# A decoder block on one core: 32 tokens by gathered expert rows in place of 16, and another order of searches, masks and dots

## The reference

```python
scores = jnp.einsum('thpk,hpnk->thpn', q, sub_keys)
v1, i1 = lax.top_k(scores[:, :, 0], PEER_TOPK)
v2, i2 = lax.top_k(scores[:, :, 1], PEER_TOPK)
best, pos = lax.top_k(cand, PEER_TOPK)            # of the sums v1 + v2
experts = (e1 * N_KEYS + e2)
gates = jax.nn.softmax(best, axis=-1)
...
u = expert_u[ic]
a = jax.nn.gelu(jnp.einsum('cd,ced->ce', xc, u), approximate=False) * gc
v = expert_v[ic]
return jnp.einsum('ce,ced->cd', a, v)
```

## Time and profile before

| | us |
|---|---|
| median of 3 runs (1616.78 to 1618.3) | 1616.78 |
| span of the profiled execution | 1615.6 |
| PE busy in it | 1607.3 |
| DVE busy | 1283.2 |
| ACT busy | 690.3 |
| V stage, first to last product | 521.6 |

### The profile page before, as it was taken

How to read it: one execution, slowest core, us unless ns; L and a number is a source line. 1 busy time by engine, 2 the same in 40 slices (tenths; PEclk the granted TensorE clock), 3 DMA queues, 4 the chain that set the end, 5 groups by cost and what they waited for, 6 DMA issues and landing times.

```text
span 1615.6 us, 25174 instructions
## 1 busy us (share of the span) xinstructions
PE 1607.3 (99%) x8581; PEld 1422.2 (88%) x8581; DVE 1283.2 (79%) x2311; ACT 690.3 (43%) x921; POOL 373.4 (23%) x286
## 2 busy tenths in 40 slices
PE   9999999999999999999999999999999999999998
PEld 7888888888888999999999999998888888888887
DVE  6855733335557999998999998778998999999997
ACT  5323433333325433334666766433334333333333
POOL 0000000000000100003322223443453555454551
PEclk9999999999999999999999999999999999999999
DMA  4332332323321656659999999998999999999994
GB/s 176 125 103 92 117 104 91 104 91 104 105 90 54 231 180 201 208 192 337 319 365 366 377 354 377 414 360 322 391 413 363 407 414 398 412 409 403 411 362 163
DMA packets 126919, 424.34 MB, mean 263 GB/s; under 512 B 16384, under 2 KB 19472, under 8 KB 125200
## 3 DMA queue, kind: packets, MB, share of 16 engines
q1 hardware_dynamic: 75168, 232.85, 39.4%
q0 software_dynamic: 39264, 142.64, 22.9%
q10 hardware_dynamic: 12432, 48.26, 7.6%
HBM read 375.18 MB, written 48.51 MB: 262 GB/s over the span
## 4 chain that ended last, share of the span: by engine, by line
PE 99%; DMA 1%; ACT 0%; DVE 0%; SPq 0%; issue 0%; ACTq 0%
PE bank L920 21%; PE bank L922 20%; PE bank L921 20%; PE bank L1102 11%; PE bank L1104 11%; PE bank L1103 11%; PE bank L1080 3%; PE bank L986 1%; DMA h_t<-x_t 1%; PE bank L967 0%; PE bank L965 0%; PE bank L966 0%; PE bank L1116 0%; PE bank L1037 0%; PE bank L938 0%; PE bank L931 0%
## 5 line engine op out<-in xcount | busy, mean ns | idle before, releaser
L1155 DVE TENSOR_TENSOR w_lo<-w_raw,w_hi 128x1024 fp32r<-128x1024 f32 x347 | 424.2, 1222 | 156.6 <-ACT w_hi L589 151.5
L589 ACT ACTIVATE w_hi<-w_raw 128x1024 fp32r<-128x1024 f32 x347 | 366.7, 1058 | 395.7 <-PE bank L1104 259.5
L920 PE MATMUL bank<-xn_hi,w_hi 128*128 128x368 f32 (+1 forms) x1472 | 516.7, 351 | 0.1
L921 PE MATMUL bank<-xn_lo,w_hi 128*128 128x368 f32 (+1 forms) x1472 | 510.9, 347 | 0.0
L922 PE MATMUL bank<-xn_hi,w_lo 128*128 128x368 f32 (+1 forms) x1472 | 510.9, 347 | 0.0
L538 POOL DMA_INDIRECT rows<-u_rows,expert x128 | 160.8, 1256 | 953.2 <-DVE expert L1555 543.2
L1102 PE MATMUL bank<-w_hi,a_hi 128*128 128x512 f32 x768 | 298.9, 389 | 0.0
L1104 PE MATMUL bank<-w_hi,a_lo 128*128 128x512 f32 x768 | 298.8, 389 | 0.0
L1103 PE MATMUL bank<-w_lo,a_hi 128*128 128x512 f32 x768 | 298.8, 389 | 0.0
L920 PEld LDWEIGHTS bank<-xn_hi,w_hi 128*128 128x128 f32 x1472 | 276.2, 188 | 17.6 <-issue 0.6
L921 PEld LDWEIGHTS bank<-xn_lo,w_hi 128*128 128x128 f32 x1472 | 276.4, 188 | 17.4 <-issue 0.2
(11 more groups left out here) (224 smaller groups left out, 1381.7 us busy)
## 6 DMA issues: line engine op xcount, KB each, us to landing
w_raw<-u SPq DMA_DIRECT2D x128, 512.0 KB
w_raw<-v SPq DMA_DIRECT2D x128, 512.0 KB
g_dram<-g_sb ACTq DMA_DIRECT2D x12, 2048.0 KB, 11.0
g_in<-g_dram SPq DMA_DIRECT2D x84, 256.0 KB
act_dram<-act_out ACTq DMA_DIRECT2D x54, 384.0 KB
act_in<-act_dram SPq DMA_DIRECT2D x54, 384.0 KB
w_raw<-gate SPq DMA_DIRECT2D x32, 512.0 KB
w_raw<-w_in SPq DMA_DIRECT2D x31, 512.0 KB
```

Source lines behind the costliest of these rows:

```text
L589: act.activation(w_hi[:, slot, :], w_raw[:, slot, :], ACT.Copy).then_inc(hi_done, 1)
L920: pe.matmul(out, hi, x_hi, start=k == 0, stop=False)
L921: pe.matmul(out, hi, x_lo, start=False, stop=False)
L1155: dve.tensor_tensor(w_lo[:, slot, :], w_raw[:, slot, :], w_hi[:, slot, :].bitcast(F32), ALU.subtract).then_inc(lo_done, 1)
```

## The change

**More gathered tokens.** EXTRA becomes 32, so the product with u has 352 columns (DU, DENSE). xn_hi and xn_lo are written for these columns alone, and act_dram holds only them. There are 32 extra gathers in place of 16. x of the extra tokens is no longer laid out by ACT: PE transposes the last 128 tokens once (8 transposes after U0), ACT copies two halves to x_last, Pool writes them to HBM 16 times over (2.1 MB) and loads them in four groups of 512 KB, two at the start and two later.

**Searches.** The order of searches follows that of the scores: one more search and one more decode stand before the U stage (10 searches in it in place of 11), and the number of w_lo at each place comes from a table, SEARCHES, through a running count (`split_tiles`). The exponentials stand after 52 gelus in place of 50.

**Masks.** e2 is cut into 8 high and 16 low values; for 32 tokens at a time (BATCH) the one-hots of both are made (512 and 256 elements), the high one is multiplied with the gates, and the columns of a mask are the product of the two over 8 x 16 = 128 keys. The first equality of 2048 elements of each mask is gone. The last two masks have three parts.

**Dots.** 2 + 14 before the rounds in place of 5 + 13, ten a round in place of nine, 28 in the plain steps as before; 56 are left for the V stage in place of 44. The extra rows are rows 10 to 41 in place of 18 to 33, and their index is read back two rows after it was stored.

```diff
-EXTRA = 16
+EXTRA = 32
...
+BATCH = 2 * MASKED
+HIGH, LOW = 8, 16
...
-DOTS_BEFORE = (1, 1, 1, 1, 1, 1, 1, 2, 1, 1, 1, 1)
-DOTS_ROUND = (1, 1, 1, 1, 1, 1, 1, 2)
...
+SEARCHES = (((4, 1, 1, 0), 0, 0), ((1, 1, 1, 0), 2, 1), ((2, 1, 1, 0), 0, 0), ((1, 1, 1, 0), 3, 0),
...
+BEFORE_FIRST = EXP_AT
+DOTS_BEFORE = (1, 2, 2, 2, 2, 3, 2)
+DOTS_ROUND = (1, 1, 1, 2, 1, 1, 1, 2)
...
-EXTRA_FIRST = DOTS_TOPK * (TOPK_STEPS // 2 - 1) + sum(DOTS_BEFORE)
+EXTRA_FIRST = DOTS_TOPK + ROW_SLOTS + 4
...
+            pool.wait_ge(x_last_ready, 2)
+            pool.dma_start(x_rows_dram, x_last[P - EXTRA:, :].unsqueeze(1).broadcast_to([EXTRA, SPREAD, D])
+                           ).then_inc(x_rows_stored, 16)
+            pool.wait_ge(x_rows_stored, 16)
+            pool.wait_ge(job_done, AT_QUERY + HALVES)
+            for g in range(X_BUFFERS):
+                load_extra(g)
             pool.wait_ge(experts_ready, 1)
...
-                if q == EXTRA_SHOWN + ROW_SLOTS:
+                if q == EXTRA_SHOWN + 2:
                     pool.wait_ge(index_stored, 16)
...
-            for b in range(SLOTS // 2):
-                gelu_tile(TOPK_STEPS, b)
+            for m in range(EXP_AT // SLOTS * SLOTS, EXP_AT):
+                gelu_tile(m // SLOTS, m % SLOTS)
             act.wait_ge(shifted, 1)
...
+            u_tile(0, 0, xn_l)
+            pe.wait_ge(scores_ready, HALVES)
+            for k in range(2):
+                for j in range(SLOTS * k, SLOTS * (k + 1)):
+                    last = pe.transpose(bank[6 + k][:, (j - SLOTS * k) * P:(j - SLOTS * k + 1) * P],
+                                        xn_full[:, j, T - P:], ident[:])
+                last.then_inc(last_turned, 1)
...
             dve.wait_ge(scores_ready, SLOTS)
-            search(0, 0, (0, 0), of(q_split, 1))
+            search(0, 0, (0, 0), turns(1, 0, 1, 0))
+            search(1, 0, (1, 0), turns(0, 1, 0, 1))
             dve.wait_ge(scores_ready, 2 * SLOTS)
-            search(0, 1, (0, 1), of(q_split, 2))
-            decode(0, 0, 0, none)
-            search(1, 0, (1, 0), [none] * SLOTS)
+            search(0, 1, (0, 1), turns(1, 0, 1, 0))
+            decode(0, 0, 0, lambda: split_tiles(1))
+            search(1, 1, (1, 1), turns(0, 0, 1, 0))
...
+            def hot_parts(batch, gates, high, gated, low, parts):
+
+
+                tokens = slice(BATCH * batch, BATCH * (batch + 1))
+                highs, lows = [P, MASKED, HIGH, 2], [P, MASKED, LOW, 2]
+                chain.did(dve.tensor_tensor(low, iota_key[:, 0:LOW, :].unsqueeze(1).broadcast_to(lows),
+                                            lanes(e2_low[:, tokens], lows), ALU.is_equal))
...
+            def mask_columns(n, held, gated, low, parts):
+
+                half = slice(n % 2 * MASKED // 2, (n % 2 + 1) * MASKED // 2)
+                shape = [P, MASKED // 2, HIGH, LOW, 2]
+                chain.wait()
                 for k in range(parts):
...
+                    last = dve.tensor_tensor(
+                        held[:, 1 + k].rearrange("p s (a b) x -> p s a b x", b=LOW),
+                        gated[:, k, half].unsqueeze(3).broadcast_to(shape),
+                        low[:, half].unsqueeze(2).broadcast_to(shape), ALU.mult)
```

More of the change, by code:

```diff
@@ L276, in build @@
         rest = MemoryMap(nc, peer.at)
+        rest_at = rest.at
         act_out = rest("act_out", [P, SLOTS, DT])
@@ L1606, in mask_gates, with lanes @@
-            def mask_gates(n, gates, held, parts):
-                shape = [P, MASKED // 2, KEYS, 2]
-                dve.wait_ge(keys_masked, n + 1)
+            def lanes(tensor, shape):
+                return tensor.rearrange("p (s x) -> p s x", x=2).unsqueeze(2).broadcast_to(shape)
+            def hot_parts(batch, gates, high, gated, low, parts):
[3 more added lines that the diff above has]
+                                            lanes(e2_low[:, tokens], lows), ALU.is_equal))
+                chain.did(dve.tensor_tensor(high, iota_key[:, 0:HIGH, :].unsqueeze(1).broadcast_to(highs),
+                                            lanes(e2_high[:, tokens], highs), ALU.is_equal))
+                chain.wait()
+                for k in range(parts):
+                    chain.did(dve.tensor_tensor(gated[:, k], high, lanes(gates[:, k], highs), ALU.mult))
@@ L1629, in extra_gates, with masks_of, mask_half @@
                 chain.wait()
+            def masks_of(n):
+                if n < MASKS - MASKS_X:
+                    return masks[n % 2], gated_hot, low_hot[:], high_hot[:], GATE_PARTS
+                return masks_x[n % 2], gated_hot_x, low_hot_x, high_hot_x, EXTRA_PARTS
+            def mask_half(n, second):
+                held, gated, low, high, parts = masks_of(n)
+                if second:
+                    mask_columns(n, held, gated, low, parts)
+                    return
+                if n >= 2:
+                    dve.wait_ge(onehots_used, SLOTS * n)
+                mask_rows(slice(MASKED * n, MASKED * (n + 1)), held)
+                if n % 2 == 0:
+                    if n > 0:
+                        dve.wait_ge(masks_ready, n)
+                    if n < MASKS - MASKS_X:
+                        gates = gate_b[:, :, BATCH * (n // 2):BATCH * (n // 2 + 1)]
+                    else:
+                        gates = gate_x[:, :, MASKED * n - DU:MASKED * n - DU + BATCH]
+                    hot_parts(n // 2, gates, high, gated, low, parts)
             def dve_round(s):
@@ L1662, in _ @@
+            chain.did(dve.tensor_copy(e2_high[:], e2_shifted[:]))
+            chain.wait()
+            chain.did(dve.tensor_copy(e2_low[:], e2_int))
+            chain.wait()
+            mask_half(0, False)
+            split_tiles(1)
+            mask_half(0, True)
+            split_tiles(1)
+            u_dots(rows_done + sum(DOTS_BEFORE[:-1]), DOTS_BEFORE[-1])
             rows_done += sum(DOTS_BEFORE)
```

272 lines of the change are left out of this document (134 added, 138 removed).

## The result

The changed kernel takes **1627.26 us** (median of 4 runs, 1625.45 to 1628.14), the kernel before 1616.93 beside it: a ratio of 1.0061, 95% interval 1.0049 to 1.0073. It is 0.6% slower, and 20 us above the forecast of 1607.

The account below looks back on a forecast made before the run. TensorE (PE), busy 1607.3 of 1615.6 us, was taken to bound the kernel. From 1615.6, -20.5 - 0.9 + 0.9 + 8.8 + 2 gave 1605.9; with the median 1.2 above the span, 1607 us, range 1597 to 1615.

Parts of the forecast that it names:

- U tile 3.84 us, -20.5: U stage: 16 dense columns less make a PE tile 3.84 us in place of 4.0, -20.5 us over 128 tiles.
- transposes -0.9: PE: 16 transposes of the extra tokens become 8, at 0.8/7 us each, -0.9 us.
- third gate part +0.9: PE: a third gate part for 16 more tokens takes 16 products more, +0.9 us.
- Searches, cost 0: One search and decode move into the query stage's DVE idle time; w_lo of U8 stays about 1 us ahead.
- The first mask, 8.8 us (4 to 13): After tile U60 PE waits for mask 0: DVE needs 39.5 us plus 5 for late rows, against 35.5.
- clock +2 (0 to 4): Behind the wait at the first mask, PE's clock falls to half for a few us: +2 us.
- D: Rounds: one-hot product at half rate, 2.2 us in place of 1.14, makes the kernel slower, 1637 us; chance 0.07.
- Rounds covered: One-hot rounds: DVE's 36.5 us a round fit within PE's 38.4, so they cost nothing.
- Plain steps, cost 0: 28 dots in 16 tiles: DVE loses some 5 of its 9 us lead; cost 0, 3 if the DMA gives less.
- The rest is hidden: Copying x of the last tokens, stores of 352 columns and ACT's fewer layouts and copies add no time.
- V stage, cost 0: DVE busy 317 of 320 us, DMA at 418 GB/s: at their edge, 9.6 us of lead covering any loss.
- rival C: V stage or plain steps fall behind too, or U8 is late: 3 to 11 us more, 1610 to 1618; chance 0.22.

Follow-up runs that it names:

- the fifth slot: Changed kernel with one more slot for the rows of v, in scratch: 1624.7 us alone, 1613.0 us with 13 rows not gathered as well.

## Why the prediction was wrong, point by point

- **U tile 3.84 us, -20.5; transposes -0.9; third gate part +0.9:** right. U60 starts 11.0 us earlier, 9.6 + 0.9 by these terms and 0.4 for what PE had lost before; from U98 to V0 it is 3.9, as the terms have it.
- **Searches, cost 0:** right. w_lo of U8 is 2.0 us ahead (I had 1), and PE has no wait up to the mask.
- **The first mask, 8.8 us (4 to 13), clock +2 (0 to 4):** right in mechanism and size, 10.6 and 1.8. Counted from the end of U51 (720.4): the split 3.7 where I had 4.0, the subtraction 4.8 (5.2), w_hi 8.9 (9.3), the product of the softmax 16.3 (16.7), the dots 31.6 without waits for rows (31.5), the mask 7.7 (8.0). The waits for rows were 6.8, not 5. (39.5 and 5 are 44.5, not the 44.3 of the text; and with waits of 8.7 to 11.7 us from trace to trace, part of the match is luck.)
- **The product of one-hots at 1.14 (D, if half rate):** 1.22 us busy. D is out. **Rounds covered:** right as long as ACT runs; no wait of PE between U62 and U94. **Plain steps, cost 0:** right, no wait of PE there.
- **"The rest is hidden":** here the first step failed. I listed the stores, layouts and copies of ACT and not extra_t, whose elements the change doubles. It cost 4.5 us. The trace of before had the warning: the issue of the store behind it took 6.37 us.
- **V stage, cost 0:** here the second step failed, and it is 13.6 of the 20 us. I had DVE's load about right as a density (317 of 320 predicted, 332.1 of 334.6 by the tile). For the stretch that I named it was wrong: that has one addition more and not 11, 112 against 111, and DVE was busy 297.3 us of it. What I made of the load was wrong too. (1) I set DVE's work and the DMA's each against PE's time, and not one on top of the other: DVE's waits for the DMA, 18.5 us, come on top of its own work. I had this as rival C and gave it 0.22. (2) I checked the rate of the DMA and not the cycle of a row slot, 10.0 to 10.2 of 10.5 us. (3) I let 9.6 us of lead cover a loss of 9.6; 8.2 of them are needed at the last three tiles, so what was really covered was 1.4. (4) 418 GB/s is about the best of the 40 slices in the earlier trace rows (419), and I took it as a mean to be had for 320 us; measured were 396, and 401 where the rows are added all the time. I had added that by the fabric ceiling of 435 GB/s in the Trainium skill (DMA: Bandwidth & Descriptors, "Where 436 GB/s comes from") the stage would fit: no stretch of the earlier trace rows or of the same table after came over 417.
- **Rival C** was right in mechanism, but its price, 3 to 11 us (0.4 to 10.4 by its own terms), stopped short: by the same 9.6 of cover, and with the 2.6 us of slow clock at the end left out.

Of the miss of 20.3 us, 13.6 are the V stage, 4.5 extra_t, and 1.6 the waits for rows and clock at the first mask. The rest, 0.6, is about what the median lies further from the profiled span than I had it, 1.9 us and not 1.2.

**Open:** in the trace after Pool stood 4.33 us before the gather of row 93 of v (1503.46), with nothing that the profile shows to wait for. The same stop, 4.31 or 4.33 us, is in the traces of all twelve variants, in some put down to DVE's addition; before, Pool has no gap over 3.14 us there. With more dots in the search stage it comes at a later row, one for each dot (row 95 with 4, 96 with 5, 101 with 10, 103 with 12, where it is 93 with 2). What it costs goes by the lead: from V102 to V108, around it, PE lost 2.7 us and DVE 1.0 of lead after; with 13 rows not gathered DVE lost 4.0 of lead, with the fifth slot as well 1.1, and with 48 dots left nothing. So up to some 4 of the 13.6 us of the V stage hang on a stop whose cause no run shows.
